# Strassen's algorithm in three more feed forward stages, and the modulation's tiles bound to ring units

## The reference

```python
def swiglu(x, w_in, w_out):
    a, b = jnp.split(x @ w_in, 2, axis=-1)
    return (jax.nn.silu(a) * b) @ w_out
...
for l in range(DEPTH):                       # DEPTH = 2
    f = swiglu(rms_norm(h, g[0]), ffn1_w_in[l], ffn1_w_out[l])
    h = h + FFN_RES * rms_norm(f, g[1])
    ...                                      # a mixer: attention and convolution, or gated linear attention
    f = swiglu(rms_norm(h, g[4]), ffn2_w_in[l], ffn2_w_out[l])
    h = h + FFN_RES * rms_norm(f, g[5])
```

## Time and profile before

| | |
|---|---|
| median of 3 runs | 1416.82 us (1416.78 to 1417.29) |
| profiled execution: time, span | 1416.94 us, 1415.1 us |
| busy: PE, PE weight loads, DVE, ACT, POOL | 1401.8, 1147.2, 956.5, 731.7, 160.1 us |
| matmuls | 7327 |
| moved by DMA | 288.24 MB, 204 GB/s in the mean |

### The profile page before, as it was taken

The page is one execution under the profiler, slowest core; times in us unless marked ns, Lnnn a source line. Parts: engine busy times, 40 slices in busy tenths (PEclk is TensorE's granted clock), DMA queues, the critical chain, the costliest instruction groups (busy, mean ns, idle before and its releaser), DMA issues.

```text
span 1415.1 us, 19090 instructions
## 1 busy us (share of the span) xinstructions
PE 1401.8 (99%) x7327; PEld 1147.2 (81%) x7327; DVE 956.5 (68%) x1307; ACT 731.7 (52%) x1050; POOL 160.1 (11%) x242
## 2 busy tenths in 40 slices
PE   9999999999999999999999999999999999999997
PEld 7888888688888888888878888888877788888886
DVE  6666567886676667665787757755568566786654
ACT  6444455564443445543665545445655634655542
POOL 1600010000000000000172100000542110011000
PEclk9999999999999999999999999999999999999999
DMA  9585755256876778868544688764845355588551
GB/s 318 199 253 198 262 203 207 68 171 207 251 242 215 231 228 265 252 210 264 187 150 148 203 210 256 255 211 140 238 160 197 121 178 179 171 242 211 178 209 59
DMA packets 234857, 288.24 MB, mean 204 GB/s; under 512 B 37076, under 2 KB 156672, under 8 KB 234768
## 3 DMA queue, kind: packets, MB, share of 16 engines
q1 hardware_dynamic: 232160, 281.48, 61.6%
q0 software_dynamic: 2208, 5.24, 1.8%
q10 hardware_dynamic: 400, 0.31, 0.1%
HBM read 282.80 MB, written 4.20 MB: 203 GB/s over the span
## 4 chain that ended last, share of the span: by engine, by line
PE 95%; DVE 2%; issue 1%; ACT 1%; POOL 0%; POOLq 0%; ACTq 0%; DVEq 0%
PE ps L706 29%; PE ps L709 28%; PE ps L707 28%; PE pst L974 1%; PE pst L1155 1%; DVE wlo L532 1%; PE pst L1468 1%; PE ps L813 0%; PE ps L812 0%; PE ps L811 0%; PE ps L1415 0%; ACT whi L521 0%; PE ps L679 0%; PE pst L1782 0%; PE pst L2355 0%
## 5 line engine op out<-in xcount | busy, mean ns | idle before, releaser
L532 DVE TENSOR_TENSOR wlo<-raw,whi 128x1024 fp32r<-128x1024 f32 (+2 forms) x468 | 558.2, 1224 | 257.7 <-ACT whi L521 255.9
L521 ACT ACTIVATE whi<-raw 128x1024 fp32r<-128x1024 f32 (+2 forms) x468 | 467.8, 1040 | 244.2 <-PE ps L709 97.4
L706 PE MATMUL ps<-whi,xh 128*128 128x512 f32 (+4 forms) x1406 | 551.5, 392 | 1.6 <-ACT xh L1013 0.6
L707 PE MATMUL ps<-wlo,xh 128*128 128x512 f32 (+4 forms) x1406 | 541.1, 385 | 0.0
L709 PE MATMUL ps<-whi,xl 128*128 128x512 f32 (+4 forms) x1406 | 532.7, 385 | 0.0
L706 PEld LDWEIGHTS ps<-whi,xh 128*128 128x128 f32 x1406 | 263.9, 188 | 60.6 <-issue 4.7
L709 PEld LDWEIGHTS ps<-whi,xl 128*128 128x128 f32 x1406 | 263.9, 188 | 53.6
L707 PEld LDWEIGHTS ps<-wlo,xh 128*128 128x128 f32 x1406 | 264.2, 188 | 49.8
L706 PE MATMUL ps<-whi,gh 128*128 128x512 f32 x440 | 172.0, 391 | 0.0
L707 PE MATMUL ps<-wlo,gh 128*128 128x512 f32 x440 | 171.2, 389 | 0.0
L709 PE MATMUL ps<-whi,gl 128*128 128x512 f32 x440 | 153.4, 389 | 0.0
(11 more groups left out here) (306 smaller groups left out, 956.0 us busy)
## 6 DMA issues: line engine op xcount, KB each, us to landing
raw<-in_ffn_w_in_dram SPq DMA_DIRECT2D x174, 512.0 KB, 5.3
raw<-in_ffn_w_out_dram SPq DMA_DIRECT2D x40, 1024.0 KB, 5.5
raw<-in_w_in_dram SPq DMA_DIRECT2D x26, 1024.0 KB, 4.8
adat<-in_w_ada_dram SPq DMA_DIRECT2D x96, 256.0 KB, 2.8
raw<-in_hyb_w_in_dram SPq DMA_DIRECT2D x10, 1024.0 KB, 5.1
raw<-in_gla_w_in_dram SPq DMA_DIRECT2D x10, 1024.0 KB, 5.2
raw<-in_w_ffn_down_dram SPq DMA_DIRECT2D x10, 1024.0 KB, 5.0
raw<-in_w_ffn_gate_dram SPq DMA_DIRECT2D x18, 512.0 KB, 3.9
```

The costliest lines, as they stand in the source:

```text
L521: e.activation(split_of(whi, j), raw_of(j), ACT.Copy).then_inc(*whi_made.up(j))
L532: e.tensor_tensor(split_of(wlo, j), raw_of(j), split_of(whi, j).bitcast(F32), ALU.subtract).then_inc(*wlo_made.up(j))
L706: e.matmul(ps[:, 0:n], a, whi_of(j, k), start=first and k == 0, stop=False)
L707: last = e.matmul(ps[:, 0:n], a, wlo_of(j, k), start=False, stop=False)
```

## The change

Stages 2, 3 and 5 are added to `STRASSEN`. Everything that asks for `st in STRASSEN` then applies to them: their order, their plan (37 units in place of 34, six of them home units), their sums and copies, and their row of gains, which is loaded into the row buffer at the down part, when p4 is split, and no longer at unit 4 of the stage. POOL gets three calls of `pool_strassen`. The modulation's units leave out the home units (119 units remain for 12 groups); the groups start every 9 or 10 of them, evenly spread, where they started every 10; and a group's sending, reading and folding stand one unit nearer to its first tile.

By this binding the tiles of stages 2 and 3 stand, among others, on 1a, 1b, 2a, 2b, p2 and 3a; those of stage 5 on 0a to 2b and again from 3b on, with a send at 3b; and the unit `U0[5] + 10` with `gate_rows`, 5a before, is now p5, so that 4a is the next load.

```diff
-        STRASSEN = (7,)
+        STRASSEN = (2, 3, 5, 7)
...
-        ada_units = [u for st in (0, 2, 3, 5) for u in range(U0[st] + (8 if st == 0 else 0), U0[st + 1])]
+        ada_units = [u for st in (0, 2, 3, 5) for u in range(U0[st] + (8 if st == 0 else 0), U0[st + 1]) if u not in home]
         ada_tiles, ada_sent, ada_read, ada_summed = {}, {}, {}, {}
         for c in range(12):
+            i = min(10 * c, c * (len(ada_units) - 13) // 11)
             for k in range(8):
-                ada_tiles[ada_units[10 * c + k]] = c, k
-            ada_sent[ada_units[10 * c + 11]] = c
-            ada_read[ada_units[10 * c + 12]] = c
-            ada_summed[ada_units[10 * c + 13]] = c
+                ada_tiles[ada_units[i + k]] = c, k
+            ada_sent[ada_units[i + 10]] = c
+            ada_read[ada_units[i + 11]] = c
+            ada_summed[ada_units[i + 12]] = c
...
             pool_open(e, 2)
+            pool_strassen(e, 2)
             pool_open(e, 3)
+            pool_strassen(e, 3)
             pool_gla(e)
             pool_open(e, 5)
+            pool_strassen(e, 5)
             pool_m2(e)
```

## The result

The changed kernel takes 1429.7 us in the median of four runs (1428.1 to 1432.18), the kernel before 1416.8 (1416.25 to 1417.29). The ratio is 1.0092 with an interval of 1.0076 to 1.0108: slower by 12.9 us. The forecast was 1426.5, in a range of 1412 to 1433. The profiled execution took 1432.18 us, with a span of 1430.3, which is 15.2 us more than the span before.

A forecast was written before the change was run, and what follows sets the result against it. TensorE was taken as the bound, busy 1401.8 of 1415.1 us, so every wait costs time. -8.2 saved + 2 x 5.9 wait in stages 2 and 3 + 6.1 in stage 5 = +9.7 us: 1426.5 us, 8-in-10 range 1412 to 1433.

The forecast's parts named there:

- The saving: Stages 2, 3 and 5: 12 matmuls fewer each, 2.72 us a stage, 8.2 us saved if nothing waits.
- Step 1: Stages 2 and 3: POOL's p1 is there at about T-3, and the gates of chunk 1 end at T+3.4.
- T: The moment when the matmuls of chunk 1 end: 1247.84 in stage 7, 517.42 in stage 3.
- Step 2: Stages 2 and 3: after x sums, splits of 2b and the add of 2a, SyncE issues 3a at T+10.7.
- Step 3: Stages 2 and 3: 6.5 us from the issue of 3a to ScalarE's first split of it, at T+17.2.
- Steps 4 and 5: Stages 2 and 3: chunk 2's gate, 5.9 us after 3a's split begins, delays chunk 3; TensorE waits 5.9 us a stage.
- the lower end of 2.6: Stages 2 and 3: chunk 1's gates at T+1.0 and 5.6 us of landing give a 2.6 us wait a stage.
- Stage 5: Waits of 0.8 us before chunk 3 and 5.3 before chunk 4, behind gate_rows: 6.1 together, between 0 and 8.
- The row of gains: Its load moves from unit 4 of the stage to the down part, some 100 us before its reading: cost zero.
- everything after the product p4: Work behind p4 in the new Strassen stages: cost zero, as the same code has slack in stage 7.
- The clock: TensorE's granted clock, 1.00 in the windows read, stays at the 2.4 GHz level.
- quick landings: Rival: 3a (stages 2, 3) and 4a (stage 5) land quickly; waits under 8.2 us, 1413.8 to 1408.6 us; chance 0.20.

The follow-up runs named there:

- Experiment 12: The kernel of experiment 8 with both gate_rows transfers as 128 pieces of 32 bytes (two gates' columns permuted): 1410.2 us, ratio 0.9953.
- Experiment 2: The changed kernel with no modulation tile on the product units such as p2: 1422.43 us, ratio 1.0038 to the kernel before.
- Experiment 6: The changed kernel with chunk 2's copy, silus and gates ahead of the splits of 3a, the x sums' low half later: 1447.31 us, ratio 1.0221.
- experiment 5: The changed kernel with the 84 later modulation adds cut to 64 of 512 columns each: 1424.66 us, ratio 1.0053.
- experiment 1: The changed kernel with gate_rows issued later, in the down part of stage 5: 1426.3 us, ratio 1.0064.
- experiment 9: The changed kernel with stage 5's gate_rows issued from ScalarE's queue at product p2 instead of SyncE's: 1427.01 us, ratio 1.007.
- experiment 10: The changed kernel with gate_rows in 128 pieces of 32 bytes instead of 1024 of 4 bytes, same place and queue: 1419.06 us, ratio 1.0018.
- Experiment 4: The changed kernel with Strassen in stage 7 only, groups' sends, reads and folds one unit nearer, tiles placed as before: 1420.46 us, ratio 1.0023.
- after: The changed kernel itself, with Strassen added in stages 2, 3 and 5: 1429.7 us, ratio 1.0092 to the kernel before.
- experiment 8: The changed kernel with no tile on p2, gate_rows moved to stage 4, and folds kept out of the openings of stages 2, 3, 5: 1413.84 us, ratio 0.998.

## Why the prediction was right, and where it was off

- **The saving** (8.2 us, 36 matmuls): the matmuls are gone. Experiment 12, which has few waits left, is 7.0 faster.
- **Step 1** (gates of chunk 1 at T+3.4): T+1.2. ScalarE splits POOL's p1 from 4.5 us after its issue, and the last packet ends after 5.0; the forecast had taken 7.4 behind 0.9 of issue.
- **Step 2** (issue of 3a at T+10.7, behind the add): T+8.5, which is T+10.7 less the 2.2 us that step 1 had too much. Experiment 2 shows that the tile on p2 is the cause.
- **Step 3** (6.5 us to the split): 5.9. The fit of the Trainium skill (page "DMA: Bandwidth & Descriptors", section "Anatomy of one DMA — SWDGE (gpsimd) path"), 4.4 us for 1 MB, is nearer to p1 of stage 2 than the forecast was (two transfers of 512 KB on POOL's path, issued at 319.38, last packet at 324.38, so 5.0), and is too short for 3a (5.9 to its split), which lands beside other transfers.
- **Steps 4 and 5** (5.9 us from the split to the gate's end; a wait of 5.9): from the split to the end of the gate's first half, which releases chunk 3, it was 5.9; the wait in its two steps was 3.06 in each stage, near the lower end of 2.6, by the 2.2 us of step 1 and the 0.6 of step 3. The mechanism was right, the size twice too large. Experiment 6 shows the order of the queues as the cause, experiment 5 that VectorE's load is not.
- **Stage 5**: 0.8 before chunk 3, measured 0.88. Before chunk 4 5.3, measured 7.33: `gate_rows` held 4a for 14.8 us in place of 12.6, but 4a was issued at T+16.4 in place of T+18.3, so its split began at T+31.1, where T+30.9 was forecast. The 2 us too few are POOL's transfer for the block sum, held as well (VectorE waits 2.07 us for it), which the forecast left out.
- **Zeros that were not zero.** The row of gains and "everything after the product p4" show no wait and stand. But stages 2 and 3 were given no wait before chunk 4, and stage 3 has 2.31 us there, by the late last packets of x2. It is not there in each profile: in experiments 1, 9 and 10, which leave stage 3 as it is, it doesn't appear. The new places of the groups, not costed at all, put a fold into the opening of stage 5: 1.65 us. Experiment 4 prices the step of one unit alone at 3.3 us in the kernel without the new Strassen stages; in after its waits (the turning behind a late gate) don't appear as such, so the two figures don't add.
- **The clock.** "The forecast leaves it there" was wrong: about 3.6 us are lost at 1.2 GHz behind the waits of 2.31 and 7.33.

So the forecast came out near partly by luck, by terms that offset each other: 5.7 us too many for two stages, and some 10 too few for `gate_rows`, the opening, the late x2 transfer and the clock. The rival "quick landings" was half right, since the landings were quick; it fell through stage 5.

## What to carry to other kernels

When a stage gets more work, follow each in-order queue for one buffer's release: here an add of 0.7 us held a load, the load a split, the split a gate, and the gate TensorE. Look for transfers of tiny pieces before making a stage tighter: one that a long look-ahead has hidden (12.6 us from a unit's issue to its split, in the rows of before) shows once that look-ahead is shorter, and moving it moves the price, while wider pieces take it away. Before a gain is put down to an edit, the profiles should be compared place by place: here 4 us in a stage that no edit touched came and went. A wait of TensorE should be priced with the slow matmuls behind it.

## What the runs showed of the hardware

- 4 KB in 1024 pieces of 4 bytes took 10.1 us in after (11.0 in before, 11.7 from ScalarE's queue) and held the loads of SyncE's and POOL's queues; in 128 pieces of 32 bytes 2.5 us in experiment 10, 4.7 in experiment 12.
- Two transfers of 512 KB on POOL's queue had nine tenths of their packets through 5.2 us after the issue, and the last one after 8.7, in stage 3 of after.
- TensorE's clock: after waits of 1.5 to 1.7 us (stages 2 and 3, and the opening of stage 5) it stayed at 2.4 GHz; after 2.31 us it was at 1.2 GHz for 3.4 us; with waits of 4.2 to 8.6 us it was for 6.8 us, of which part lies within the wait; with 9.35 us for 10.2. The length of a wait alone does not tell: after 1.70 us in stage 4 (experiment 8) it was at 1.2 GHz for 3.4 us, and after 2.90 us in stage 7 (experiment 6) it stayed at 2.4.
- TensorE waited 1.7 us for "issue" (experiment 8) while the small pieces were moved, and no longer with wide ones. A packet of 16 KB of instructions took 3.4 us there in place of 1.0. What TensorE lacked, the trace doesn't name.
